# One decoder step: the triangular inverses of a group merged as two streams of two matrices

## The reference, cut to what matters

```
def step(S, inp):
    r_t, d_t, k_t, v_t, kk_t, a_t = inp
    sa = einsum('bhvk,bhk->bhv', S, kk_t)
    S = S * d_t[:, :, None, :] - sa[..., None] * (kk_t * a_t)[:, :, None, :] \
        + v_t[..., None] * k_t[:, :, None, :]
    return S, einsum('bhvk,bhk->bhv', S, r_t)
S, y = lax.scan(step, s0, (r, decay, k, v, kk, a))
```

## Time and profile before

| | us |
|---|---|
| median of 3 runs (4345.37 to 4363.92) | 4346.11 |
| the profiled execution | 4364.41 |
| its span, from first to last instruction | 4362.9 |
| the recurrence with its 120 merges, by its first and last X and Z | 702 to 1406 |

### The profile page before, as it was taken

One profiled execution on the slowest core, in us unless ns is written; L12 is line 12 of the kernel. 1 busy time (PEld: TensorE's weight loads), 2 busy tenths in 40 slices (PEclk: granted clock), 3 DMA queues, 4 the chain that ended last, 5 costly groups with the idle time before them and its releaser, 6 DMA issues. The chain is left out here.

```text
span 4362.9 us, 65680 instructions
## 1 busy us (share of the span) xinstructions
PE 3796.4 (87%) x22546; PEld 3486.4 (80%) x22546; DVE 3222.2 (74%) x6195; ACT 1185.2 (27%) x2093; POOL 1226.0 (28%) x1054
## 2 busy tenths in 40 slices
PE   7997757888888569782776999999999999999997
PEld 6997644777778565552776999999999999999997
DVE  5421554565753337887996999999999999999998
ACT  3212232231311112212993222222222222222221
POOL 0221000000000000000003565555555555555553
PEclk8998666888987789986998999999999999999998
DMA  4774120000000300010347888888888888888885
GB/s 92 86 86 101 52 90 23 19 11 19 11 8 1 116 21 22 33 49 2 166 205 280 299 293 294 294 292 297 291 296 290 297 291 299 288 299 284 305 289 195
DMA packets 292099, 729.43 MB, mean 167 GB/s; under 512 B 27528, under 2 KB 138840, under 8 KB 290448
## 3 DMA queue, kind: packets, MB, share of 16 engines
q0 software_dynamic: 120560, 431.42, 32.0%
q1 hardware_dynamic: 171424, 296.57, 20.0%
HBM read 650.20 MB, written 77.70 MB: 167 GB/s over the span
## 5 line engine op out<-in xcount | busy, mean ns | idle before, releaser
L2502 POOL DMA_INDIRECT experts_u_row<-in_up_rows,experts_u_at x384 | 534.6, 1392 | 645.2 <-DVE experts_dot L2688 525.2
L107 PE MATMUL experts_down_ps<-experts_act_hi,experts_down_hi 128*128 128x352 f32 x2048 | 676.5, 330 | 10.8 <-DVE experts_down_lo L2664 8.3
L107 PE MATMUL experts_up_ps<-experts_u_hi,experts_up_hi 128*128 128x352 f32 x2048 | 661.8, 323 | 27.5 <-DVE experts_u_lo L2664 26.4
L108 PE MATMUL experts_up_ps<-experts_u_lo,experts_up_hi 128*128 128x352 f32 x2048 | 660.8, 323 | 0.0
L109 PE MATMUL experts_up_ps<-experts_u_hi,experts_up_lo 128*128 128x352 f32 x2048 | 660.6, 323 | 0.0
L108 PE MATMUL experts_down_ps<-experts_act_lo,experts_down_hi 128*128 128x352 f32 x2048 | 660.5, 323 | 0.0
L109 PE MATMUL experts_down_ps<-experts_act_hi,experts_down_lo 128*128 128x352 f32 x2048 | 659.8, 322 | 0.0
L2509 POOL DMA_INDIRECT experts_v_row<-in_down,experts_v_at x384 | 519.6, 1353 | 242.4 <-issue 104.2
L2688 DVE CUSTOM_DVE_ANT_0 experts_u_row<-experts_u_row,stream_u_rows_of 128x1024 f32<-128x1024 f32 x384 | 466.5, 1215 | 70.5 <-DMA experts_u_row<-in_up_rows,experts_u_at 69.1
L2701 DVE SCALAR_TENSOR_TENSOR stream_h_rows_of<-experts_v_row,experts_weight,stream_h_rows_of 128x1024 f32<-128x1024 f32 x384 | 497.8, 1297 | 12.6 <-DVE experts_weight L2693 6.8
L2707 DVE TENSOR_TENSOR stream_h<-stream_h,experts_down_ps 128x704 f32<-128x704 f32 x512 | 450.6, 880 | 71.6 <-PE experts_down_ps L109 67.3
(11 more groups left out here) (380 smaller groups left out, 6614.1 us busy)
## 6 DMA issues: line engine op xcount, KB each, us to landing
experts_up<-in_up SPq DMA_DIRECT2D x128, 512.0 KB
experts_down<-in_down SPq DMA_DIRECT2D x128, 512.0 KB
gates<-spread_spread SPq DMA_DIRECT2D x11, 4096.0 KB
experts_gates<-gates SPq DMA_DIRECT2D x64, 704.0 KB
cols<-inp_done POOLq DMA_DIRECT2D x27, 576.0 KB
inp_w_in<-in_w_in SPq DMA_DIRECT2D x27, 512.0 KB
pick_w_query<-in_w_query SPq DMA_DIRECT2D x16, 512.0 KB, 4.0
experts_u_row<-in_up_rows,experts_u_at POOLq DMA_INDIRECT x384
```

The costliest lines, as they stand in the source:

```text
L107: pe.matmul(out, w_hi, x_hi, start=start, stop=False)
L108: pe.matmul(out, w_hi, x_lo, start=False, stop=False)
L2502: pool.indirect_dma_start(u_row[b][:], None, up_rows_d, bass.IndirectOffsetOnAxis(ap=u_at[slot][:, b, a:a + 1], axis=0)).then_inc(u_row_lo ...
```

## The change

The matrices of a group are split in two halves, `w` = 0 and 1, of `n` matrices each (two of the four; one of the two in group 0). A half is the two heads of one tile. Each half has a PSUM bank of its own, `half_ps[w]`, that holds both its X (columns 0 to 255) and its Z (256 to 511), where before one bank held X and one held Z of all. The four semaphores count halves instead of merges. TensorE writes X of half 0, then X of half 1, later Z of half 0 and Z of half 1, each half with its own wait; ScalarE copies and VectorE adds half by half. The number and the size of the matmuls stay; ScalarE has two copies of 256 columns instead of one of 512, VectorE two adds of 128 columns for each of 256. The points and what stands at them stay.

```
-        x_ps, z_ps, chain_ps = psum("x_ps", BANK), psum("z_ps", BANK), psum("chain_ps", BANK)
+        half_ps, chain_ps = [psum(f"half_ps_{w}", BANK) for w in range(2)], psum("chain_ps", BANK)
...
+        def halves(group, l, w):
+            return ((group.i * MERGES + l) - 1) * 2 + w + 1
...
                 def merge(group, l, after, at_point, prepare_next):          # ScalarE
-                    act.wait_ge(x_done, group.i * MERGES + l)
-                    act.activation(neg_x[:, 0:group.m, :], x_quads(group.m), ACT.Copy, scale=-1.0).then_inc(x_ready, 1)
+                    for w in range(2):
+                        act.wait_ge(x_done, halves(group, l, w))
+                        act.activation(neg_x[:, w * group.n:(w + 1) * group.n, :], x_half(w, group.n), ACT.Copy, scale=-1.0).then_inc(x_ready, 1)
...
-                    dve.wait_ge(z_done, group.i * MERGES + l)                # VectorE
-                    if l < LEVELS - 1:
-                        t = half_cols(inv[:, 0:m, :], l, 0)
-                        dve.tensor_tensor(t, t, pieces(0), ALU.add)
-                    t = half_cols(inv_t[:, 0:m, :], l, 1)
-                    dve.tensor_tensor(t, t, pieces(1), ALU.add).then_inc(merged, 1)
+                    for w in range(2):
+                        dve.wait_ge(z_done, halves(group, l, w))
+                        of_half = slice(w * n, w * n + n)
+                        pieces = [z_half(w, which, n).rearrange("p m (a w) -> p m a w", w=1 << l) for which in range(2)]
+                        if l < LEVELS - 1:
+                            t = half_cols(inv[:, of_half, :], l, 0)
+                            dve.tensor_tensor(t, t, pieces[0], ALU.add)
+                        t = half_cols(inv_t[:, of_half, :], l, 1)
+                        dve.tensor_tensor(t, t, pieces[1], ALU.add).then_inc(merged, 1)
...
-                    pe.wait_ge(merged, k0 - 1)                               # TensorE
-                    for i in range(m):
-                        mm = pe.matmul(x[:, i, :], join[:, i, :], inv[:, i, :], start=True, stop=True)
-                    mm.then_inc(x_done, 1)
+                    for w in range(2):
+                        if group.i or l > 1:
+                            pe.wait_ge(merged, halves(group, l, w) - 2)
+                        for i in range(n):
+                            mm = pe.matmul(x_half(w, n)[:, i, :], join[:, w * n + i, :], inv[:, w * n + i, :], start=True, stop=True)
+                        mm.then_inc(x_done, 1)
                     at_point(l - 0.5)
                     prepare_next()
-                    pe.wait_ge(x_ready, k0)
+                    for w in range(2):
+                        pe.wait_ge(x_ready, halves(group, l, w))
...
```

35 lines of the change are left out of this document (17 added, 18 removed).

## The result

The changed kernel takes 4281.03 us (median of 4 runs, 4278.02 to 4287.81), the kernel before beside it 4351.73: a ratio of 0.9831, 95% interval 0.9814 to 0.9848, 71 us less by the medians, 73 by the ratio. I had forecast 40 us. The kernel before ran 5.6 us slower here than the 4346.11 that the forecast started from; from the same start the miss of the range would be 7 us. Two later comparisons of the same change gave 0.9824 [0.9799, 0.9848] and 0.9833 [0.9814, 0.9851], so the prediction's sign was right and its size was not.

What follows compares the result with a forecast made beforehand. TensorE was taken as the bound, with 81.6 us idle and a 0.86 clock to gain from. Savings of 28 us direct and 12 us clock, 40 together, came off the median, giving 4306 us; range 4282 to 4342.

Steps and rivals of the forecast that it cites:

- direct, merges at full clock: In the merges, halves shorten TensorE's idle time before X and Z: 28 us saved, bounds 13 to 46.
- clock in the merges: Closing short gaps avoids some falls of TensorE's clock to 1.2 GHz: 12 us saved, bounds nothing to 26.
- that difference of 19: Three lower-clock stretches behind short gaps, 41 us together, would take about 22 us at the upper level.
- 0.72 us saved: Behind level 5, the last X record starts 0.72 us earlier, and a gap of 0.22 us stays.
- What comes back: Gain lost where TensorE's next wait ends with a VectorE chain: 5 to 6 us taken off the direct sum.
- That the waits cost TensorE: Rival: 240 added waits cost TensorE 0.21 us each, 50 us, making it 22 us slower, 4368; chance 0.07.
- That VectorE takes it back: Rival: merges' gains are lost at later waits that VectorE ends; only 13 us remain, 4333; chance 0.18.
- The clock "all": Rival: the clock gives its full 26 us besides 28 direct, 54 us in all, 4292; chance 0.13.
- VectorE's added work: Splitting 220 adds costs VectorE 0.06 us each, 13 us, on the path only in late merges.
- The marks that I had named: Signs in the profile after: stage idle 82 to some 55 us, shorter X and Z waits, clock 0.88 or above.

Runs made afterwards that it cites:

- repeated kernel before: The kernel before, unchanged, run and profiled once more: ratio 0.9999 to the kernel before.
- the kernel before with its long waits filled: The kernel before plus 110 unread unit-matrix matmuls in TensorE's long waits for VectorE, short gaps left open: ratio 0.9937 to the kernel before.
- both joined: The changed kernel, but ScalarE's copies and VectorE's adds wait for the second half before beginning the first: ratios 0.9902 and 0.9906 to the kernel before.
- Filling the short gaps: The kernel before plus unread unit-matrix matmuls in most of TensorE's short gaps, behind Z and between X and Z: ratio 0.9941 to the kernel before.
- long fills and the change together: The changed kernel plus 110 unread unit-matrix matmuls in TensorE's remaining long waits: ratios 0.9805 and 0.9793 to the kernel before.

## Why the prediction was wrong

The sum was 28 + 12 = 40 us. The runs put it like this:

| term | forecast | measured |
|---|---|---|
| direct, merges at full clock (608 to 572) | 28 (13 to 46) | 36 |
| clock in the merges ((176 - 125) / 2) | 12 (0 to 26) | 25 |
| clock at the end of the stage, outside the merges | none | about 5 |
| picking stage | none | 7 |
| sum | 40 | 73; the three ratios are worth 72 to 77 |

**The step that failed** is the size of the clock's term, and with it the assumption that the rest of the program stays as it is. "I take 12 us, some two thirds of that difference of 19" priced only falls behind the short gaps of the earlier trace rows. The difference of the means is 25 us, nearly the end of the bounds. Three mistakes lie in it. I tied falls to the gaps right ahead of them, and the same gaps stand ahead of no fall in two of three places of the repeated kernel before, and of none at 764 to 790 us in the kernel before with its long waits filled. I made the gain hang on closing these gaps, and the kernel with both joined has it without the overlap. And I let one profile stand for a kernel whose time at the lower level is between 150 and 195 us from execution to execution. By the eight profiles alone the 25 us are known only to some 14; the granted clocks of all executions put the clock's share of the whole program, merges and end of the stage, at 32 and 29 us, each known to some 10. What the clock hangs on is not the sum of idle time either: both joined had 79 us idle and 106 at the lower level, the changed kernel 53 idle and 116 to 137. Filling the short gaps and filling the long waits each took as much off (78 and 76 us over the whole span); long fills and the change together took 116, their single effects (76 and 58) would be 134, which can't be told apart. Which sequence of gaps makes a fall, I could not settle.

**The direct term** was mis-sized by 8 us, within its bounds. The idle time fell by 31 us (mean 83.6 to 53.0), near my figure. The other 5 us or so I put down to the overlap of 0.17 us with the tail of the last matmul, which every gap hides and which I left out: the profiles have 110 gaps of TensorE in the merges before the change and 64 after it, and 46 times 0.17 is 8 us, against which stands the wait of half 1 inside X. This is an estimate; no run takes it apart. At level 5 I had 0.72 us saved; it was 0.94 and 0.17, less 0.32 within X, so 0.79. What comes back was right: the mask's wait grew from 14.1 to 16.4 us, level 1 of group 4 from 0.56 to 1.83 in two places, some 5 us.

**Outside the merges** I said that "nothing in it says that the stage at hand is the cause" of the slower profile and took it that the rest of the program stays. The end of the stage, from the last Z on, lasted 34.9 to 35.1 us in all five profiles with the schedule of before, at a clock of 0.60, and 28.8, 32.8 and 28.8 us in the three of the changed kernel (33.9 and 34.0 with both joined). The second of the three:

```profile
1339.80:1372.60 32.80, 14.76 (x64) 10.25 (x63) 16.67 (x16) 4.40 (x10) 1.08 (x2) 0.64 0.01 2
```

And the picking stage lost its pauses. Neither was in the sum or the range. Inside the merges the change gave 36 + 25 = 61 us; taken from the median of before, 4346 or 4352, that would still lie inside the range. With these 12 us the time fell below it.

**The rivals.** That the waits cost TensorE is refuted: no idle time of TensorE ahead of X is put down to issue, its weight loads show less of it than before, and both joined, which has all of the added waits, needs 604.5 us at full clock, less than before. That VectorE takes it back (13 us direct) is refuted by the 36. The clock "all" (54 us in sum) was the nearest case and still too small; its price of 26 us for the clock was about right, for a reason that the runs don't bear out.

**VectorE's added work** was on the path as little as I had said. Its busy time rose by 21.9 us (396.4 to 418.3) for 220 more adds, 0.10 each, of which 0.04 overlap with the next. The rule that I had weighed against the change, the fixed cost of small tiles in the Trainium skill (VectorE: DVE Perf Modes, section "The TRN2 errata — SBUF-src ops pay a fixed extra latency per instruction"), gave an estimated 27 us. The trace agrees roughly with that size as busy time; as time of the kernel it is nothing, since VectorE still waits 181 us for Z.

**The marks that I had named** came out: idle from 82 to 52 (forecast 55); Z's wait to 0.2 (1 to 2); X's to 27.0, where 13 for `inv_t` and 11.5 for `join` had been forecast, 24.5 together; the mask's wait 2.3 us longer, that of L1481 (L1486 after) 1.2 shorter; clock 0.91 (0.88 or above).

## What to carry to other kernels

When an engine is handed back and forth between others, split each batch in two with a wait for each half: the consumer's first half then lies beside the producer's second. Do it on every hop; here adds and copies gave 20 and 14 us and hardly shared anything. Then test what else came with the split: here a kernel with the halves and no overlap kept more than half of the gain. Where TensorE still must wait for longer than a few matmuls, and its clock is at the lower level for a fifth of a stage, matmuls that nobody reads can be worth more than they cost; try it beside the kernel on one chip, and price the clock from several executions of one kernel, never from one profile. And compare all the stages of two profiles, not only the changed one.

## What the runs showed of the hardware

- A gap between matmul records hides more than it shows: four records of Z last 0.61 us, but the successor, which waits for nothing, starts 0.44 us after their start.
- The time at TensorE's lower level in 700 us of merges was 150 to 195 us over five executions of the schedule of before, at idle times between 81.6 and 85.2. With both joined it was 106.3 and 106.0 in two profiles, but the granted clock of its ten executions over the whole span goes from 0.918 to 0.923, which is 659 to 706 us at the lower level: it scatters too.
- VectorE paused for 1.4 to 1.5 us three times in a stage, put down to issue, behind the jump back of a loop; with 20, 110 or 220 more instructions ahead of them it did not. 20 memsets that compute nothing are worth 7 us in that stage, so an edit of VectorE's program can add or remove as much in a loop far behind it; more instructions on TensorE alone changed nothing there (423.4 us).
